# A chunked gated recurrence in a four-branch decoder layer: the small products of two neighbouring blocks put in one row

## What is computed

```python
def _hgrn2(q, f_pre, i, lb, norm_g):
    ...
    k = (1.0 - lb) * jax.nn.sigmoid(-f_pre)
    log_f = jnp.log1p(-k)
    ...
    def step(S, inp):
        q_c, k_c, v_c, lf_c = inp
        b = jnp.cumsum(lf_c, axis=2)
        rel = jnp.where(causal, b[:, :, :, None, :] - b[:, :, None, :, :], -jnp.inf)
        scores = jnp.sum(q_c[:, :, :, None, :] * k_c[:, :, None, :, :] * jnp.exp(rel), -1)
        o = (jnp.einsum('bhts,bhsv->bhtv', scores, v_c)
             + jnp.einsum('bhtk,bhkv->bhtv', q_c * jnp.exp(b), S))
        b_end = b[:, :, -1:, :]
        S = (jnp.exp(b_end)[:, :, 0, :, None] * S
             + jnp.einsum('bhsk,bhsv->bhkv', k_c * jnp.exp(b_end - b), v_c))
        return S, o
    ...
merged = sum(merge_gates[:, :, b_i] * (branches[b_i] @ w_branch[l, b_i]) for b_i in range(N_BRANCH))
```

## Time and profile before

| | us |
|---|---|
| median of 3 runs | 1095.77 |
| lowest and highest of them | 1094.17, 1098.38 |
| the profiled execution | 1097.14 |
| its span in the trace | 1095.0 |
| TensorE busy with matmuls in that span | 1058.5 (97%) |
| branch B's blocks, first transposes to the end of the last update | 732.7 to 876.5 |

### The profile page before, as it was taken

The page is one execution under the profiler, slowest core; times in us unless marked ns, Lnnn a source line. Parts: engine busy times, 40 slices in busy tenths (PEclk is TensorE's granted clock), DMA queues, the critical chain, the costliest instruction groups (busy, mean ns, idle before and its releaser), DMA issues.

```text
span 1095.0 us, 22343 instructions
## 1 busy us (share of the span) xinstructions
PE 1058.5 (97%) x9736; PEld 830.6 (76%) x9736; DVE 592.4 (54%) x976; ACT 304.9 (28%) x497; POOL 373.6 (34%) x343
## 2 busy tenths in 40 slices
PE   7999999999999799999999999999999999999997
PEld 5686787767677677877877777877778777888885
DVE  3768933976455152353442118557777586423543
ACT  5545113321502102202201034244545341001221
POOL 1431543321435421222222232344334239762000
PEclk9999999999999899999999999999999999999999
DMA  9700111210110110110111121120101026412221
GB/s 355 263 21 10 48 49 49 77 29 25 40 28 25 34 41 26 35 41 25 35 41 31 30 68 39 39 59 26 51 26 50 26 86 246 129 36 96 96 77 58
DMA packets 80129, 70.25 MB, mean 64 GB/s; under 512 B 4128, under 2 KB 68896, under 8 KB 80032
## 3 DMA queue, kind: packets, MB, share of 16 engines
q1 hardware_dynamic: 74560, 49.35, 14.6%
q10 hardware_dynamic: 5472, 19.47, 4.8%
HBM read 64.61 MB, written 4.19 MB: 63 GB/s over the span
## 4 chain that ended last, share of the span: by engine, by line
PE 84%; DVE 9%; POOL 3%; DMA 1%; ACT 1%; issue 1%; SPq 1%; ACTq 0%; DVEq 0%; POOLq 0%
PE bank L590 52%; PE bank L1123 8%; PE bank L639 6%; PE bank L691 2%; PE bank L1078 1%; DVE slots L1706 1%; DMA slots<-in_w_mod 1%; PE bank L910 1%; PE bank L915 1%; DVE tab L1924 1%; PE bank L796 1%; DVE stage L1917 1%; PE bank L860 1%; POOL y_lo L476 1%; DVE slots L1690 1%
## 5 line engine op out<-in xcount | busy, mean ns | idle before, releaser
L590 PE MATMUL bank<-hn_hi,w_hi 128*128 128x512 f32 x880 | 360.9, 410 | 10.4 <-POOL w_lo L507 7.6
L590 PE MATMUL bank<-hn_hi,w_lo 128*128 128x512 f32 x880 | 344.6, 392 | 0.0
L590 PE MATMUL bank<-hn_lo,w_hi 128*128 128x512 f32 x880 | 344.6, 392 | 0.0
L505 POOL CAST w_hi<-w_raw 128x512 fp32r<-128x512 f32 x110 | 86.1, 783 | 537.1 <-PE bank L590 537.1
L590 PEld LDWEIGHTS bank<-hn_hi,w_hi 128*128 128x128 f32 x880 | 165.8, 188 | 51.8 <-issue 12.5
L590 PEld LDWEIGHTS bank<-hn_hi,w_lo 128*128 128x128 f32 x880 | 165.9, 189 | 36.4
L590 PEld LDWEIGHTS bank<-hn_lo,w_hi 128*128 128x128 f32 x880 | 166.2, 189 | 33.2 <-issue 1.9
L507 POOL TENSOR_TENSOR w_lo<-w_raw,w_hi 128x512 fp32r<-128x512 f32 x110 | 155.4, 1413 | 8.8
L1257 ACT ACTIVATE stage<-bank 128x512 f32<-128x512 f32 x64 | 38.2, 600 | 208.0 <-PE bank L590 189.4
L1861 DVE TENSOR_TENSOR stage<-stage,bank 128x512 f32<-128x512 f32 x48 | 33.0, 687 | 50.2 <-PE bank L639 48.9
L1235 ACT ACTIVATE slots<-bank 128x512 f32<-128x512 f32 x42 | 24.6, 599 | 123.0 <-PE bank L590 122.9
(11 more groups left out here) (320 smaller groups left out, 1546.5 us busy)
## 6 DMA issues: line engine op xcount, KB each, us to landing
w_raw<-in_w_in SPq DMA_DIRECT2D x110, 256.0 KB, 2.8
slots<-in_w_mod SPq DMA_DIRECT2D x16, 512.0 KB, 11.4
slots<-in_x SPq DMA_DIRECT2D x8, 512.0 KB, 9.5
w_branch<-in_w_branch SPq DMA_DIRECT2D x32, 128.0 KB, 2.8
slots<-in_w_mod ACTq DMA_DIRECT2D x8, 512.0 KB, 5.2
slots<-in_w_out ACTq DMA_DIRECT2D x8, 512.0 KB, 6.3
xr<-in_x ACTq DMA_DIRECT2D x8, 512.0 KB, 3.5
out<-xr ACTq DMA_DIRECT2D x8, 512.0 KB, 2.6
```

What stands on the lines that cost most here:

```text
L505: nc.gpsimd.tensor_copy(w_hi[p][:, :, :], w_raw[p][:, :, :]).then_inc(s_pool_step, 1)
L590: last = mm(o, w[p][:, k4, :], h[:, k, n * HALF:(n + 1) * HALF], start=(p == 0 and k4 == 0 and q == 0), stop=(p == 1 and k4 == 3 and q == 2))
```

## The change

On TensorE the products of a block are regrouped. The code of the scores and of the output and update become functions, and the loop runs output and update of block i and then at once the scores of block i + 1, with all ten pieces of big products in one `fill(10)` before them. The `fill(1)` between the two halves of line 1078 is gone. Within the scores the 96 finest products come first and the 64x64 and the other 32x32 products last, behind a wait for the output that was just issued (both write bank 7). The update of the last block, whose result nobody reads, is left out. The number of pieces is 77 before (seven blocks of ten, and 1 + 4 + 2) and 77 now (seven of ten, 5 and 2).

On ScalarE the copy of block i's output moves behind the copies of block i + 1's scores, and the exponentials of block i + 2 move to the end of block i, behind the sigmoid of the gate tile. On VectorE the update of S with block i's products moves to the start of block i + 1, before the masks.

```diff
-            for i in range(NT):
-                ts = slice(i * P, (i + 1) * P)
+
+            def b_scores(i):
                 pe.wait_ge(s_b_z_ready, i + 1)
-                if i:
-                    pe.wait_ge(s_b_o_ready, i)
-                    pe.wait_ge(s_b_s_ready, 2 * i + 1)
-                    pe.wait_ge(s_b_p_ready, 10 * i)
                 zd = dz[i % 2]
...
                 for j in range(2):
-                    if j == 1:
-                        fill(1)
                     for l in range(NLOW):
                         for nb in range(4):
                             for hh, r in enumerate(halves):
...
+                if i:
+                    pe.wait_ge(s_b_o_done, i)
+                for j in range(2):
+                    for hh, r in enumerate(halves):
+                        c0 = 320 + j * 64
+                        mm(bank[6 + hh][0:64, c0:c0 + 64], zd[r, 0, j, 0:64], zd[r, 0, j, 64:128], start=True, stop=True)
...
                 last.then_inc(s_b_scores_done, 1)
-                fill(4)
+
+            def b_output(i):
                 pe.wait_ge(s_b_p_ready, 10 * i + 10)
                 pe.wait_ge(s_b_s_ready, 2 * i + 1)
+                if i:
+                    pe.wait_ge(s_b_o_ready, i)
...
                 last.then_inc(s_b_o_done, 1)
+
+            def b_update(i):
                 pe.wait_ge(s_b_ke_ready, i + 1)
...
                 last.then_inc(s_b_snew_done, 1)
-                fill(5 if i + 1 < NT else 2)
-            pe.wait_ge(s_b_s_ready, 17)
+
+            b_scores(0)
+            for i in range(NT):
+                fill(10 if i + 1 < NT else 5)
+                b_output(i)
+                if i + 1 < NT:
+                    b_update(i)
+                    b_scores(i + 1)
+            fill(2)
...
+            decay_factors(1)
             for i in range(NT):
-                if i + 1 < NT:
-                    act.wait_ge(s_b_d_ready, i + 2)
-                    zd = dz[(i + 1) % 2]
-                    nc.scalar.activation(zd[:, :, :, :], zd[:, :, :, :], ACT.Exp).then_inc(s_b_e_ready, 1)
-                    after(s_b_e_ready)
...
-                act.wait_ge(s_b_o_done, i + 1)
...
+                if i:
+                    b_output(i - 1)
                 if i + 1 < NT:
                     merge_gate()
+                if i + 2 < NT:
+                    decay_factors(i + 2)
+            b_output(NT - 1)
...
             for i in range(NT):
+                if i:
+                    dve.wait_ge(s_b_snew_done, i)
                 dve.wait_ge(s_b_scores_done, i + 1)
+                if i:
+                    for j in range(2):
+                        nc.vector.scalar_tensor_tensor(out=h_s[:, j * 64:(j + 1) * 64],
...
-                dve.wait_ge(s_b_snew_done, i + 1)
```

More of the change, by code:

```diff
@@ L1079, in _ @@
                                           stop=True, tile_position=(64 * hh, 32 * nb))
+                if i:
[5 more added lines that the diff above has]
+                for j in range(2):
+                    for nb in (0, 2):
+                        for hh, r in enumerate(halves):
+                            c0 = 256 + j * 32
+                            last = mm(bank[6 + hh][32 * nb:32 * nb + 32, c0:c0 + 32], zd[r, 1, j, 32 * nb:32 * nb + 32],
+                               zd[r, 1, j, 32 * nb + 32:32 * nb + 64], start=True, stop=True,
+                               tile_position=(64 * hh, 32 * nb))
                 last.then_inc(s_b_scores_done, 1)
-                fill(4)
+            def b_output(i):
                 pe.wait_ge(s_b_p_ready, 10 * i + 10)
                 pe.wait_ge(s_b_s_ready, 2 * i + 1)
+                if i:
+                    pe.wait_ge(s_b_o_ready, i)
                 for h in range(4):
@@ L1452, in _, with decay_factors, b_output @@
             hp4 = h_p.rearrange("p (j o) t -> p o j t", o=2)
-            for i in range(NT):
-                if i + 1 < NT:
-                    act.wait_ge(s_b_d_ready, i + 2)
-                    zd = dz[(i + 1) % 2]
-                    nc.scalar.activation(zd[:, :, :, :], zd[:, :, :, :], ACT.Exp).then_inc(s_b_e_ready, 1)
-                    after(s_b_e_ready)
+            def decay_factors(i):
+                act.wait_ge(s_b_d_ready, i + 1)
+                zd = dz[i % 2]
+                nc.scalar.activation(zd[:, :, :, :], zd[:, :, :, :], ACT.Exp).then_inc(s_b_e_ready, 1)
+                after(s_b_e_ready)
+            def b_output(i):
+                act.wait_ge(s_b_o_done, i + 1)
+                nc.scalar.activation(pair(14)[:, :, i * P:(i + 1) * P],
+                                     bank[7][:, 0:256].rearrange("p (j t) -> p j t", j=2), ACT.Copy)\
+                    .then_inc(s_b_o_ready, 1)
+                act.wait_ge(s_b_o_ready, after(s_b_o_ready))
+            decay_factors(1)
+            for i in range(NT):
                 act.wait_ge(s_b_scores_done, i + 1)
@@ L2089, in _ @@
             for i in range(NT):
+                if i:
+                    dve.wait_ge(s_b_snew_done, i)
                 dve.wait_ge(s_b_scores_done, i + 1)
+                if i:
+                    for j in range(2):
+                        nc.vector.scalar_tensor_tensor(out=h_s[:, j * 64:(j + 1) * 64],
+                                                       in0=h_s[:, j * 64:(j + 1) * 64],
+                                                       scalar=e_last[(i - 1) % 2][:, j:j + 1],
+                                                       in1=bank[4][:, 384 + j * 64:448 + j * 64], op0=MUL,
+                                                       op1=ADD).then_inc(s_b_s_ready, 1)
                 for hh in range(2):
```

## The result

The changed kernel takes **1108.43 us** (median of 4 runs, 1107.03 to 1111.92) where the kernel before took 1095.66 in the same comparison (1094.17 to 1098.38). The ratio is 1.0115, with an interval of 1.0097 to 1.0132: slower by 1.2%, or 12.8 us. The forecast was 1100.5 with a range of 1093 to 1108: the direction was right, the size was not, and the median lies 0.4 above the range.

A forecast was written before the change was run, and what follows sets the result against it. TensorE's own row of work was taken as the bound. Change-overs and last update -3.5, old holes -3.3, new holes +11.5 gave +4.7 us on 1095.77: 1100.5 us, 8-in-10 range 1093 to 1108.

The forecast's parts named there:

- the holes' cause: TensorE, finest scores: holes lie where a new 256-instruction program packet begins, used up faster than the next arrives; four old, 3.3 us.
- the places 168, 72, 232, 136, (40), 200 and 104: Instruction in each of branch B's seven stretches where the first packet border was counted to fall; the second 256 later.
- Their price: New holes in branch B's seven stretches were to cost +11.5 us, lower end 7, upper 21.7.
- the price of 2.0: Cost in us of a hole in a stretch holding a whole packet: old hole 0.41 plus the removed 1.60 piece.
- the first rival: Hidden refills: packet crossings are mostly hidden, so no new holes come and old ones go; 1089.0 us, chance 0.13.
- The change-overs: TensorE's returns to big products: 15 fewer at 0.22 us save 3.3; with the last update dropped (0.23), -3.5 us.
- the new seams: Seams between kinds of small product, as many in another order: 0 +- 0.1 us in each of seven stretches, +-0.7.
- The clock: Rival: TensorE's clock falls after stretches without big products; 26 us on top for seven (1126), two 1108; chance 0.07.
- The forecast's own sign of being wrong: In branch B, a granted clock under 1.00 between 733 and 880 us would show the forecast wrong.
- VectorE and ScalarE at nothing: Their reordered work in branch B was to cost TensorE nothing, with VectorE's 3.12 us of idle time as cover.
- the regrouping buys its change-overs and no more: Rival: holes only where weight loads delay a packet, some four of 0.8 us; 1092.3, up to 1096; chance 0.10.

The follow-up runs named there:

- moved borders: Already-reached waits added in TensorE's big-product fills, shifting packet borders: changed kernel, borders at stretch front 1141.41 us or mid-scores 1154.88; kernel before, borders at front 1131.37.
- two pieces: Two pieces of big products between the halves of the finest scores: kernel before 1093.04 us (0.9969), changed kernel 1092.94 us (0.9971).
- the borders in the middle: Changed kernel plus already-reached waits in seven fills, 12 in the first and 160 later, putting packet borders mid finest scores: 1154.88 us, ratio 1.0521.
- the kernel before with moved borders: Kernel before plus already-reached waits among its big products, putting packet borders at the front of each half of the finest scores: 1131.37 us, ratio 1.0311.
- borders at the front: Changed kernel plus already-reached waits in seven fills, 140 in the first and 160 later, putting packet borders at each stretch's front: 1141.41 us, ratio 1.0402.

## Why the prediction missed, point by point

**What bounds the kernel, and the holes' cause: right.** TensorE alone sets the pace, the gaps are packet borders, and the experiments with moved borders and with two pieces agree. One reading on the way was off: the packet of the earlier trace rows does not move just ahead of the end of the 1.51 us hole, but at 754.3, 0.8 us before the hole begins and 2.3 before it ends. The other three gaps before and the six after end 2.3 to 2.4 us after the start of such a packet as well, so the link holds with that distance. The distances from gap to gap in the changed kernel (columns as the earlier trace rows):

```profile
755.01:775.58 20.57, 19.19 (x254) 0.92 0.12 33
775.58:796.24 20.66, 19.73 (x382) 1.00 0.12 35
796.24:814.90 18.66, 16.88 (x255) 1.00 0.13 37
814.90:855.01 40.11, 38.50 (x636) 0.96 0.12 35
855.01:874.32 19.31, 17.36 (x255) 1.00 0.12 36
```

The counts stand as 2 to 3 to 2 to 5 to 2 packets, which is what the places 168, 72, 232, 136, (40), 200 and 104 give with 608 instructions a block.

**Their price: right.** I took 11.5 us for seven stretches and 10.4 at the price of 2.0; it was 10.5:

| border at | 168 | 72 | 232 | 136 | 40 | 200 | 104 |
|---|---|---|---|---|---|---|---|
| forecast, at 2.0 | 2.0 | 1.3 | 1.4 | 2.0 | 0 | 1.7 | 2.0 |
| measured | 2.85 | 1.38 | 0.93 | 1.78 | 0 | 1.61 | 1.95 |

The rule used, old gap plus the piece that had covered it, holds within half a microsecond, but for the first. That the sum at the price of 2.0 comes out within 0.1 is in part luck: the first gap was 0.85 dearer, the third and the fourth together 0.7 cheaper. The first packet was asked for while weights were still coming in; the share of the DMA engines in 40 slices from 750 to 757, in tenths:

```profile
DMA  0001535999994230000000000000000000030000
```

and the only packet of any queue from 752.6 to 755.1:

```profile
q8 instruction: 1, 0.02, 2.4%
```

The engines are nearly full until about 752.1; the packet moves at 752.6, and the gap ends 2.4 us later, as at the other five. By the count of places TensorE had passed the border at 168 some 1.6 us before that move, against 0.6 to 0.9 us in stretches 3, 4, 6 and 7 (an estimate from the count and the chain). So what is longer in the first gap lies ahead of the packet's move. That the weight loads hold it up was argued in the forecast for the old gap and is not tested here. The Trainium skill, "Runtime: NRT & Kernel Launch", section "Instruction fetch mechanics", says that such a crossing is mostly hidden. Of 77 packets most are, here too; the trace shows six in branch B that are not, and the first rival, built on that rule, falls.

**The change-overs: right in kind, too large.** -3.5 forecast, -2.3 measured. A block without a gap lost 0.32 us and not 2 x 0.22 = 0.44. I had put the new seams at nothing, give or take 0.1 each; this term was mis-sized. The transposes behind the update of S take 0.37 where behind big products they took 0.22: 0.15 more in each of seven stretches.

**The clock: this step failed.** It stood in the text as a rival with a chance of 0.07, at a price for all seven stretches or for two in a larger form (3.7 us each), and the forecast itself carried nothing for it. Two things were wrong. First, "against it" I held that the clock had stayed at 1.00 through block 1 with its hole of 1.51, and that the array works in two thirds of the new stretch. Neither bore on gaps beyond 1.51, while I forecast four of 1.7 to 2.0 and allowed up to 3.1; the only rows with a longer idle time, showed a fall. Over all kernels here the clock fell behind none of the gaps in branch B up to 1.61 us, and behind 8 of the 10 from 1.78 to 2.85 (three of three in the changed kernel, five of seven with the borders in the middle). Second, it isn't an alternative to the forecast but comes *on top of* it, stretch by stretch. The forecast's own sign of being wrong, a clock under 1.00 between 733 and 880, is what came. The price of one was 1.3, 1.6 and 1.3 us, well under the 3.7 of the earlier trace rows. Had I added half of four such falls at 1.4, the forecast would have been 1103, and its upper end some 1111.

Put together, branch B by the steps of the sum: forecast -3.5 - 3.3 + 11.5 = +4.7; measured -2.3 - 3.3 + 10.5 + 4.2 = +9.1. The difference is the clock, 4.2, with 1.2 from the change-overs and -1.0 from the holes nearly cancelling. What the median misses beyond that is 1.2 outside branch B, where 1.64 is again a fallen clock, and the 2.6 that the spans don't hold.

**VectorE and ScalarE at nothing: right.** No wait of TensorE in the branch names them, in any of the kernels with the new order. The rival "the regrouping buys its change-overs and no more" falls with the six gaps.

**Left open:** at which gap exactly the clock falls (2.08 did nothing twice, 1.78 did it once); what holds the packet of the first gap up; whether the 1.64 us behind branch B are the change's; and where the rest of the 2.6 us between medians and spans lies.

## What to carry to other kernels

Small products use up an engine's program fast: count the instructions between two pieces of long work, and where some 256 of them pass in less than a refill takes (here 1.27 us against about 3.3, an estimate by 1.27 + 1.60 + 0.41 of the earlier trace rows and 1.27 + 1.95 of the changed kernel's last gap), long work among them is no interruption but the cover of the next packet. Regrouping that saves 0.3 us a block can so cost 1.5 us a block, and a gap of about 2 us in TensorE's row should be priced with the slow products behind it. Here two pieces of six big products between the halves did better than one (0.9971 to 0.9996 of before, in the changed order) or none (1.0115).

## What the runs showed of the hardware

- Waits for semaphores that have long been reached are free between TensorE's big products only while they are few. With five of them behind each product, 18 products took 4.32 us as against 4.31 without (the kernel before with moved borders, from 743.75); with seven the products start some 0.34 us apart instead of 0.2267, with nine 0.44 (borders at the front, first fill). There they made the block, from the first fill to the end of the next stretch, 24.2 us long (734.70 to 758.93) where a block without a gap has 18.0.
- The clock went to its lower level behind 8 of 10 gaps of 1.8 to 2.9 us between small products, and stayed there for some 3 us of work (755.0 to 758.5 in stretch 1), in which the 64x64 products took 0.62 us for 0.38 and the big ones started 0.43 us apart.
- The packets are so regular that the gaps could be placed beforehand by counting instructions, and moved by adding them: seven gaps of 2.02 to 2.63 us with the borders in the middle of the finest scores, none with the borders at the front.
